# A decoder's mixer and sliding attentions: half weight tiles spread over eight steps, three engines' programs reordered, and the sliding attention's output product started beside its last units

## The chip, the cores and the metric

The kernel runs on one core of a Trainium2 chip. The core has five engines that run their own programs and wait for each other by semaphores: TensorE (matmuls; PE in the profile, its weight loads PEld), VectorE (DVE), ScalarE (ACT), GpSimd (POOL) and SyncE (SP, which here issues the weight loads from memory). The metric is the device time of one execution in microseconds (us), the median of the runs of one kernel.

## What is computed

Two transformer blocks on 256 tokens of width 1024, all in 32-bit floats, with one weight matrix after the other streamed from memory. Two of its parts matter here. First the mixer's attention:

```python
def hybrid_mixer(h, w_in, ...):
    ...
    o_nsa = nsa_attention(...)                    # 8 heads, 2 groups of keys, selected + window + compressed keys
    o_fox = forgetting_attention(...)             # 8 heads, a bias that decays with distance
    y = jax.nn.sigmoid(gate_a) * (o_nsa @ w_up_nsa) + jax.nn.sigmoid(gate_b) * (o_fox @ w_up_fox)
    return y @ w_out
```

Here `gate_a` and `gate_b` are columns of `h @ w_in`, that is, products that don't depend on the attention. Second the sliding attention of the last layer:

```python
def swa_layer(h, k_sh, v_sh, wq, q_gain, sinks, wo):
    q = rms_norm((h @ wq).reshape(B, T, N_Q_HEADS, HEAD_DIM), q_gain) * (HEAD_DIM ** -0.5)
    return swa_sink_attention(q, k_sh, v_sh, sinks) @ wo
```

## The kernel before

**Weights.** They come in tiles of 256 columns or rows, 1 MB each, into a ring of four places (`feed`, issued by SyncE). Each half tile (128 x 1024) is split into a rounded part, which ScalarE copies out of the ring (`tile_hi`, L294), and the rest, which VectorE subtracts (`tile_lo`, L304). There are four places for split halves, so a half can be split once the half four before it has been multiplied. A product takes three matmuls (L344 to L346), and a half tile 24 of them. `heads_after` and `rests_after` issue such splits for all halves whose place is free once a given half is done.

**Attention.** `attention_stage` runs over units (four lanes of scores for 128 queries). There are 12 units in the mixer: four with 128 keys and four with 256 keys of the first kind, then two with 128 keys and two with 256 of the second. The sliding attention has four units with 128 keys and four with 256. The stage is a software pipeline: in step s the engines do

- TensorE: scores of unit s, transposes of the weights of unit s-2 (L979), values of unit s-3
- VectorE: scores plus bias and their maximum for unit s (in the text: combine), division by the sums for unit s-1 (L1063), the store of unit s-3's output as a pair of parts (L338, L339)
- ScalarE: exponentials of unit s (L1005), and the copy of unit s-2's transposed weights out of PSUM (L1022)

Each engine goes through its steps in the order in which they are written. In the mixer the last four tiles of the gates ride along as fillers, because TensorE has little to do in an attention: one whole tile of 48 matmuls in each of steps 0 to 3, between the scores and the transposes, copied out by ScalarE (L1011). One wait sets the pace around them: TensorE starts a filler only when the one before is copied.

`ahead` is the step at which the splits for the section that follows are issued. At the end of the stage stands a barrier of all engines (`nc.Block`, L929), and then `up_stage` in the mixer, or `out_stage` (`row_to_T`, four tiles into PSUM banks 4 to 7) after the sliding attention.

Of the kernel before, what the change touches and what calls it, by code (L numbers as in the profile page):

```python
# [23 lines left out]
P = 128  # L24
SEQ = 256
# [354 lines left out]


def col_to_natural(e, pe, g, src, bank):
# [11 lines left out]
def row_to_T(e, pe, g, src, k0, first, last):  # L394


    def chunk(w, k, m):
        return product(pe, e.ps[:, 4 + m // 2, span(m % 2, SEQ)], cut(w, ALL, span(m, P)), cut(src, ALL, k0 + k, ALL),
                       first and k == 0 and m % 2 == 0, last and k == 1 and m % 2 == 1)
# [86 lines left out]

def add_to_residual(e, dve, b, scale, last_tile):

# [5 lines left out]
    if scale == 1.0:  # L494
        x = dve.tensor_tensor(xs, e.ps[:, 4 + b, :], xs, ALU.add)  # L495
    else:
        x = dve.scalar_tensor_tensor(out=xs, in0=e.ps[:, 4 + b, :], scalar=scale, in1=xs, op0=ALU.mult, op1=ALU.add)
    x.then_inc(*e.sig("residual_added").one())
# [10 lines left out]

def tail_vector(e, dve, scale, outs, last_tile):  # L510


    for n in range(6 if outs else 4):
        if n < 4:
            add_to_residual(e, dve, n, scale, last_tile)
        if outs and n >= 2:
# [394 lines left out]

def attention_stage(e, units, follows, fillers=(), hT=None, beside=None):

# [10 lines left out]
         "values_ready", "values_stored", "filler_copied", "dve_step"))  # L924
    last_tile = max([g for g, _ in fillers], default=-1)
    DEPTH = min(3, n)
    ahead = min(len(fillers) + 1, n - 1) + beside.delay

    with nc.Block() as block, ExitStack() as stack:  # L929
        tag = nc.next_id()  # L930
# [20 lines left out]
        def _(pe):  # L951
            for step in range(n + 3):
# [30 lines left out]
                if 0 <= u < n:  # L983
# [9 lines left out]
                    for mm in lasts:  # L993
                        mm.then_inc(*values_ready.one(2 // len(lasts)))

        @block.scalar
        def _(act):
            for step in range(n + 2):
                if beside:
                    beside.first_scalar(act, step)  # L1000
                if step < n:
                    act.wait_ge(*max_ready.at(step + 1))
                    st = stat[:, step % 2]
                    for lane in range(4):
                        x = act.activation(summed(step)[:, lane], summed(step)[:, lane], ACT.Exp,  # L1005
                                           bias=st[:, 0, lane:lane + 1], accum_out=st[:, 1, lane:lane + 1])
                    x.then_inc(*sums_ready.one())
                if step < len(fillers):
                    g, dst = fillers[step]
                    tile_after(e, act, g)  # L1010
                    act.activation(dst, e.ps[:, 7, :], ACT.Copy).then_inc(*filled.one())  # L1011
                if step == ahead:
                    heads_after(e, act, 2 * follows)
                u = step - 2
                if u >= 0:
# [5 lines left out]
                    src = e.ps[:, 4:6, :].rearrange("p b n -> p (b n)")[:, 0:width]  # L1021
                    act.activation(pT[:, u % 2, 0:width], src, ACT.Copy).then_inc(*copied.one())  # L1022

        @block.vector
        def _(dve):
            link = Chain(dve, dve_chain)
            for step in range(n + 3):
# [16 lines left out]
                if beside:  # L1044
                    beside.vector(dve, step)
                if step < len(fillers):
                    rests_before(e, dve, fillers[step][0] + 1)
                if step == ahead:
# [18 lines left out]
                if 0 <= u < n:  # L1067
                    dve.wait_ge(*values_ready.at(2 * (u + 1)))
                    units[u].store(link, out_ap(u)).then_inc(*stored.one())

def mixer_section(e):
    nc = e.nc
    with ExitStack() as stack:
# [24 lines left out]
                        + [fox_unit(e, m, t, j) for t in range(TT) for j in range(2)], FIRST["up"],  # L1101
                        fillers=[(FIRST["gates"] + n - 1, m.ab[:, 2 * n + 2:2 * n + 4, :].rearrange("p m n -> p (m n)"))
                                 for n in range(FILLERS, 7)], hT=e.hT, beside=front)
        memory.raw, memory.sq = e.sq, queries
# [1886 lines left out]
def swa_section(e, kvT):  # L2991
    with ExitStack() as stack:
# [8 lines left out]
        last = swa_projections(e, s, kvT)  # L3001
        attention_stage(e, [swa_unit(e, s, t, j) for t in range(TT) for j in range(4)], FIRST["wo2"], beside=last)
        out_stage(e, "wo2", s.o, [("ln_mlp1", e.hT)])

# [407 lines left out]
```

## Time and profile before

| what | us |
|---|---|
| median of 3 runs | 1501.92 (1501.85 to 1503.39) |
| the profiled execution, its own time | 1512.18 |
| its span, first to last instruction | 1510.9 |
| mixer's attention, first scores to the first matmul of the up section | 312.75 to 393.06 |
| sliding attention, first scores to the first matmul of its output product | 1244.6 to 1295.36 |
| the output product's 192 matmuls | 1295.36 to 1318.63 |

The profile shows one execution. TensorE is busy for 94% of the span, so most of the kernel is bound by its matmuls; the two attentions are the places where it idles, and the change concerns only them.

### The profile page before, as it was taken

What the parts mean: (1) busy time and instruction counts of PE and PEld (TensorE: products, weight loads), DVE (VectorE), ACT (ScalarE), POOL (GpSimd) and SP (SyncE); (2) the same over time, 40 slices, a digit from 0 to 9 for tenths busy, and PEclk for the clock granted to TensorE, in tenths of its full rate; (3) what the DMA queues carried; (4) which work ended last, traced back from release to release, by engine and by line L of the source; (5) the groups of instructions that cost most, each with busy time, mean ns of one, the idle gap of its engine ahead of it and who ended that gap; (6) DMA issues with size and microseconds to landing.
All of it is one profiled execution on the core that took longest, in us unless ns stands there. A gap on an engine that the chain in (4) does not pass through costs nothing. (4 is left out here: it accounts for less than half of the span.)

```text
span 1510.9 us, 28880 instructions
## 1 busy us (share of the span) xinstructions
PE 1420.5 (94%) x12748; PEld 1361.9 (90%) x12748; DVE 951.8 (63%) x1303; ACT 713.4 (47%) x1096; POOL 7.1 (0%) x12
## 2 busy tenths in 40 slices
PE   7999999997899999999989978998999996889999
PEld 7999999895799899999988977888999984889999
DVE  4655666468675456555678864566656678466565
ACT  5444454355464455444538423444444555454443
POOL 0000000000000000000000010000000000000000
PEclk9999999998999999999989986999999997999999
DMA  6555545640344334555514300023554530335542
GB/s 256 205 196 185 183 154 196 250 169 1 131 177 168 126 126 168 198 193 172 191 57 171 140 3 30 29 85 140 183 207 168 196 112 1 140 140 189 202 168 84
DMA packets 33108, 222.47 MB, mean 147 GB/s; under 512 B 3879, under 2 KB 5295, under 8 KB 6616
## 3 DMA queue, kind: packets, MB, share of 16 engines
q1 hardware_dynamic: 31928, 219.57, 40.3%
q8 instruction: 100, 1.64, 0.4%
q10 hardware_dynamic: 1056, 1.07, 0.2%
q14 instruction: 24, 0.20, 0.0%
HBM read 219.54 MB, written 1.07 MB: 146 GB/s over the span
## 5 line engine op out<-in xcount | busy, mean ns | idle before, releaser
L304 DVE TENSOR_TENSOR tile_lo<-ring,tile_hi 128x1024 fp32r<-128x1024 f32 x396 | 476.1, 1223 | 321.9 <-ACT tile_hi L294 321.2
L294 ACT ACTIVATE tile_hi<-ring 128x1024 fp32r<-128x1024 f32 x396 | 408.3, 1054 | 293.4 <-PE ps L346 289.3
L344 PE MATMUL ps<-hT_hi,tile_hi 128*128 128x256 f32 x1664 | 472.7, 284 | 10.1 <-DVE hidden_lo L753 7.6
L345 PE MATMUL ps<-hT_lo,tile_hi 128*128 128x256 f32 x1664 | 469.1, 282 | 0.0
L346 PE MATMUL ps<-hT_hi,tile_lo 128*128 128x256 f32 x1664 | 468.8, 282 | 0.0
L344 PEld LDWEIGHTS ps<-hT_hi,tile_hi 128*128 128x128 f32 x1664 | 316.0, 190 | 16.6 <-DVE hidden_lo L753 8.0
L346 PEld LDWEIGHTS ps<-hT_hi,tile_lo 128*128 128x128 f32 x1664 | 316.2, 190 | 0.0
L345 PEld LDWEIGHTS ps<-hT_lo,tile_hi 128*128 128x128 f32 x1664 | 315.9, 190 | 0.0
L344 PE MATMUL ps<-hidden_hi,tile_hi 128*128 128x256 f32 x864 | 241.5, 280 | 0.0
L346 PE MATMUL ps<-hidden_hi,tile_lo 128*128 128x256 f32 x864 | 241.5, 280 | 0.0
L345 PE MATMUL ps<-hidden_lo,tile_hi 128*128 128x256 f32 x864 | 241.5, 280 | 0.0
L346 PEld LDWEIGHTS ps<-hidden_hi,tile_lo 128*128 128x128 f32 x864 | 164.1, 190 | 0.0
L345 PEld LDWEIGHTS ps<-hidden_lo,tile_hi 128*128 128x128 f32 x864 | 162.9, 188 | 0.0
L344 PEld LDWEIGHTS ps<-hidden_hi,tile_hi 128*128 128x128 f32 x864 | 162.2, 188 | 0.0
L709 ACT ACTIVATE hidden_hi<-hidden_whole 128x512 fp32r<-128x512 f32 x54 | 34.1, 632 | 116.2 <-DVE hidden_whole L740 67.3
L753 DVE TENSOR_TENSOR hidden_lo<-hidden_whole,hidden_hi 128x512 fp32r<-128x512 f32 x54 | 37.4, 692 | 40.6 <-ACT hidden_hi L709 30.6
L1005 ACT ACTIVATE scores<-scores,lane_stats 128x128 f32<-128x128 f32 (+3 forms) x80 | 35.5, 445 | 47.0 <-DVE lane_stats L1043 46.9
L979 PEld LDWEIGHTS ps<-const_sb,scores 128*128 128x128 f32 x120 | 17.7, 178 | 33.7 <-issue 25.7
L979 PE MATMUL ps<-const_sb,scores 128*128 128x128 f32 x120 | 23.1, 346 | 26.5 <-ACT weightsT L1022 18.2
L746 DVE TENSOR_TENSOR hidden_whole<-gate,token_scale 128x512 f32<-128x512 f32 x32 | 22.2, 693 | 37.5 <-ACT gate L706 37.5
L706 ACT ACTIVATE gate<-ps 128x512 f32<-128x512 f32 x32 | 19.1, 597 | 47.6 <-PE ps L346 47.6
L344 PE MATMUL ps<-y_turned,tile_hi 128*128 128x256 f32 x128 | 36.2, 283 | 1.9 <-DVE tile_lo L304 1.9
(459 smaller groups left out, 2134.9 us busy)
## 6 DMA issues: line engine op xcount, KB each, us to landing
ring<-stream SPq DMA_DIRECT2D x204, 1024.0 KB, 4.8
x_sb<-x SPq DMA_DIRECT2D x4, 256.0 KB, 4.1
bias<-f_dram ACTq DMA_DIRECT2D x1, 1024.0 KB, 8.2
fox_bias<-forget_dram SPq DMA_DIRECT2D x1, 1024.0 KB, 6.2
squares<-mem SPq DMA_DIRECT2D x1, 1024.0 KB, 4.8
out<-x_sb SPq DMA_DIRECT2D x4, 256.0 KB, 2.2
const_sb<-const SPq DMA_DIRECT2D x1, 577.0 KB, 9.6
small_sb<-small SPq DMA_DIRECT2D x1, 493.5 KB, 9.7
```

The lines of the kernel that those rows point to most:

```text
L294: act.activation(e.w_hi[:, n % SPLIT, :], e.ring[:, tile % RING, span(n % 2, HALF)], ACT.Copy).then_inc(e.tile_hi.handle, 1)
L304: dve.tensor_tensor(e.w_lo[:, n % SPLIT, :], e.ring[:, CUT[n // 2] % RING, span(n % 2, HALF)], e.w_hi[:, n % SPLIT, :].bitcast(F32), ALU.s ...
L344: pe.matmul(out, left[0], right[0], start=start, stop=False)
L345: pe.matmul(out, left[0], right[1], start=False, stop=False)
L346: return pe.matmul(out, left[1], right[0], start=False, stop=stop)
L706: act.activation(tmp[:, j % 2, :], e.ps[:, 2 * (j % 2), :], ACT.Relu).then_inc(*act_done.one())
L709: act.activation(slot(hid[0], j), whole[:, j % 2, :], ACT.Copy).then_inc(*hi_ready.one())
L746: link.done(dve.tensor_tensor(halves_of(both), halves_of(tmp[:, j % 2, :]), scale_pairs(e), ALU.mult))
L753: dve.tensor_tensor(slot(hid[1], j), both, slot(hid[0], j).bitcast(F32), ALU.subtract).then_inc(*hidden_ready.one())
L979: tr = pe.transpose(e.ps[:, 4 + at // 512, at % 512:at % 512 + P], s[:, u % DEPTH, lane, kb * P:(kb + 1) * P], const(e, "ident"))
L1005: x = act.activation(summed(step)[:, lane], summed(step)[:, lane], ACT.Exp, bias=st[:, 0, lane:lane + 1], accum_out=st[:, 1, lane:lane + 1])
```

## The change

In the mixer the fillers become eight half tiles in steps 0 to 7, and TensorE does its half tile at the end of a step, behind the values. ScalarE's step is turned around: copy of the last filler, copy of the transposed weights, one split, and then the exponentials. VectorE's split moves to the end of its step. `attention_stage` is shared, so ScalarE's new order holds in the sliding attention too.

```diff
@@ attention_stage, tensor @@
-                if step == len(fillers) and step >= 1:
-                    pe.wait_ge(*filled.at(step))
-                if step < len(fillers):
-                    if step >= 1:
-                        pe.wait_ge(*filled.at(step))
-                    col_to_T(e, pe, fillers[step][0], hT, 7)
...
+                if tail and step >= n:
+                    if step == n:
+                        pe.wait_ge(*max_ready.at(n))
+                    tail.tensor(pe, step - n)
+                if step == len(fillers) and step >= 1:
+                    pe.wait_ge(*filled.at(step))
+                if step < len(fillers):
+                    if step >= 1:
+                        pe.wait_ge(*filled.at(step))
+                    g, half, _ = fillers[step]
+                    half_col_to_T(e, pe, g, half, hT, 7)
@@ attention_stage, scalar @@
+                if 1 <= step <= len(fillers):
+                    g, half, dst = fillers[step - 1]
+                    multiplied(e, act, g, half)
+                    act.activation(dst, e.ps[:, 7, span(half, SEQ)], ACT.Copy).then_inc(*filled.one())
+                u = step - 2
+                if u >= 0:
+                    act.wait_ge(*turned.at(u + 1))
...
+                    act.activation(pT[:, u % 2, 0:width], src, ACT.Copy).then_inc(*copied.one())
+                if step < len(fillers):
+                    g, half, dst = fillers[step]
+                    heads_after(e, act, 2 * g + half)
                 if step < n:
                     act.wait_ge(*max_ready.at(step + 1))
@@ attention_stage, vector @@
-                if step < len(fillers):
-                    rests_before(e, dve, fillers[step][0] + 1)
...
                     units[u].store(link, out_ap(u)).then_inc(*stored.one())
+                if step < len(fillers):
+                    rests_after(e, dve, 2 * fillers[step][0] + fillers[step][1])
```

After the sliding attention the first three half tiles of the output product `wo2` are multiplied in the drain of the pipeline, steps 8 to 10, one behind the values of each step; they need only the units whose outputs are already stored. They go to banks 0 to 3, which the last scores have left, and the barrier between the two is gone (`Open` instead of `nc.Block`). The rest follows in a new `swa_output`:

```diff
+class SlidingOutput:
...
+    def half_tile(self, pe, i, k):
+        e = self.e
+        pe.wait_ge(*self.stored.since(5 + i))
+        w = arrived(e, pe, FIRST["wo2"] + i, k)
+        for m in range(KC):
+            mm = product(pe, e.ps[:, m // 2, span(m % 2, SEQ)], cut(w, ALL, span(m, P)), cut(self.o, ALL, 2 * i + k, ALL),
+                         i == 0 and k == 0 and m % 2 == 0, False)
+        mm.then_inc(*e.tile_done.one())
+
+    def tensor(self, pe, n):
+        self.half_tile(pe, n // 2, n % 2)
@@ swa_output @@
+            for n in range(3, 6):
+                rest.tensor(pe, n)
+            pe.wait_ge(*stored.since(8))
+            row_to_T(e, pe, g0 + 3, s.o, 6, False, True, 0)
```

The changed order, at three places. ScalarE in the mixer, from the exponentials of unit 0 on, before:

```order
L294 ACTIVATE tile_hi<-ring 128x1024
L1011 ACTIVATE gates_ab<-ps 128x512
L1005 ACTIVATE scores,lane_stats<-scores,lane_stats 128x128 x4
L294 ACTIVATE tile_hi<-ring 128x1024 x2
L1011 ACTIVATE gates_ab<-ps 128x512
L1022 ACTIVATE weightsT<-ps 128x512
L1005 ACTIVATE scores,lane_stats<-scores,lane_stats 128x128 x4
```

and in the changed kernel (its lines have other numbers; `gates_ab` is the copied filler):

```order
L1018 ACTIVATE gates_ab<-ps 128x256
L294 ACTIVATE tile_hi<-ring 128x1024
L1035 ACTIVATE scores,lane_stats<-scores,lane_stats 128x128 x4
L1018 ACTIVATE gates_ab<-ps 128x256
L1027 ACTIVATE weightsT<-ps 128x512
L294 ACTIVATE tile_hi<-ring 128x1024
L1035 ACTIVATE scores,lane_stats<-scores,lane_stats 128x128 x4
```

A step now has one split instead of two, in front of the exponentials instead of behind them, and the copy of the transposed weights has moved in front of them as well.

VectorE in the mixer, around the end of step 3 and step 4, before:

```order
L1536 TENSOR_TENSOR scores<-ps,bias 128x2x128 x2
L1043 TENSOR_REDUCE lane_stats<-scores 128x4
L304 TENSOR_TENSOR tile_lo<-ring,tile_hi 128x1024 x2
L1054 RECIPROCAL lane_stats<-lane_stats 128x4
L1058 TENSOR_TENSOR lane_stats<-lane_stats,gate_nsa 128x4
L1063 TENSOR_SCALAR scores<-scores,lane_stats 128x128 x4
```

and in the changed kernel:

```order
L1553 TENSOR_TENSOR scores<-ps,bias 128x2x128 x2
L1060 TENSOR_REDUCE lane_stats<-scores 128x4
L1069 RECIPROCAL lane_stats<-lane_stats 128x4
L1073 TENSOR_TENSOR lane_stats<-lane_stats,gate_nsa 128x4
L1078 TENSOR_SCALAR scores<-scores,lane_stats 128x128 x4
L338 CAST o_parts<-ps 128x128
L339 TENSOR_TENSOR o_parts<-ps,o_parts 128x128
L304 TENSOR_TENSOR tile_lo<-ring,tile_hi 128x1024
```

The subtraction for the split has moved from between the maximum and the division to the end of the step.

TensorE at the end of the sliding attention (transposes L979, values L3224), before:

```order
L979 MATMUL ps<-const_sb,scores 128x128 x8
L3224 MATMUL ps<-weightsT,v_swa 64x128 x8
L979 MATMUL ps<-const_sb,scores 128x128 x8
L3224 MATMUL ps<-weightsT,v_swa 64x128 x16
L929 UNCONDITIONAL_BRANCH
```

and in the changed kernel, from the first half tile's last matmul (there are 24 matmuls in front of these rows that read `o_swa`):

```order
L346 MATMUL ps<-o_swa_hi,tile_lo 128x256
L982 MATMUL ps<-const_sb,scores 128x128 x8
L3293 MATMUL ps<-weightsT,v_swa 64x128 x8
L344 MATMUL ps<-o_swa_hi,tile_hi 128x256
...
L346 MATMUL ps<-o_swa_hi,tile_lo 128x256
L3293 MATMUL ps<-weightsT,v_swa 64x128 x8
L344 MATMUL ps<-o_swa_hi,tile_hi 128x256
```

A half tile of the output product now stands between the values of unit 5 and the transposes of unit 7, one between the values of units 6 and 7, and there is no branch to a barrier.

## Rows read from the trace of the kernel before

**Rows 1.** The page, busy time (share of the span) and instructions.

```profile
PE 1420.5 (94%) x12748; PEld 1361.9 (90%) x12748; DVE 951.8 (63%) x1303; ACT 713.4 (47%) x1096; POOL 7.1 (0%) x12
```

**Rows 2.** Stretches of the mixer: length, PE, PEld, DVE, ACT, POOL busy, PEclk, DMA.

```profile
312.75:340.83 28.08, 28.00 (x246) 26.42 (x245) 17.02 (x32) 16.57 (x45) 0.00 (x0) 1.00 0.40 146
340.83:366.50 25.67, 16.85 (x122) 11.42 (x120) 21.14 (x55) 11.76 (x38) 0.00 (x0) 0.73 0.00 1
366.50:393.06 26.56, 17.84 (x172) 13.63 (x173) 18.59 (x53) 13.34 (x41) 0.00 (x0) 0.87 0.00 1
354.00:362.00 8.00, 5.65 (x28) 3.77 (x28) 6.98 (x20) 2.75 (x10) 0.00 (x0) 0.50 0.01 2
```

**Rows 3.** Waits, 312 to 394: who for whom, total us, times, longest.

```profile
DVE tile_lo L304 <- ACT tile_hi L294: 13.8, 5, 3.1
PE ps L979 <- ACT weightsT L1022: 9.8, 7, 2.9
```

**Rows 4.** Timeline of VectorE, mixer: start, us, operation [idle before].

```profile
315.13 0.73 DVE L1536 TENSOR_TENSOR scores<-ps,bias 128x256 f32<-128x256 f32 x2
315.90 0.69 DVE L1043 TENSOR_REDUCE lane_stats<-scores 128x4 f32<-128x512 f32 x1
319.26 1.23 DVE L304 TENSOR_TENSOR tile_lo<-ring,tile_hi 128x1024 fp32r<-128x1024 f32 x1 [2.67 <-ACT tile_hi L294]
...
356.70 1.28 DVE L1536 TENSOR_TENSOR scores<-ps,bias 128x512 f32<-128x512 f32 x2
...
359.15 0.17 DVE L1054 RECIPROCAL lane_stats<-lane_stats 128x4 f32<-128x4 f32 x1
...
360.61 0.29 DVE L338 CAST o_parts<-ps 128x128 fp32r<-128x128 f32 x1
...
366.50 0.76 DVE L1581 TENSOR_TENSOR scores<-ps,cmp_in 128x256 f32<-128x256 f32 x2
```

**Rows 5.** Timeline of ScalarE, mixer.

```profile
323.46 2.00 ACT L294 ACTIVATE tile_hi<-ring 128x1024 fp32r<-128x1024 f32 x2
326.04 0.60 ACT L1011 ACTIVATE gates_ab<-ps 128x512 f32<-128x512 f32 x1 [0.59 <-PE ps L346]
329.52 0.40 ACT L1005 ACTIVATE scores<-scores,lane_stats 128x128 f32<-128x128 f32 x1 [2.88 <-DVE lane_stats L1043]
...
361.25 1.00 ACT L1022 ACTIVATE weightsT<-ps 128x1024 f32<-128x1024 f32 x1
```

**Rows 6.** Timeline of TensorE, mixer.

```profile
344.96 1.13 PE L1530 MATMUL ps<-k_sel_win,queries 64*128 64x256 f32 x8
...
367.72 1.06 PE L979 MATMUL ps<-const_sb,scores 128*128 128x128 f32 x8 [1.26 <-ACT weightsT L1022]
368.71 1.09 PE L1546 MATMUL ps<-weightsT,v_sel_win 128*64 128x128 f32 x16
369.74 0.43 PE L1548 MATMUL ps<-cmp_weightsT,cmp_v 15*64 15x128 f32 x4
```

**Rows 7.** Busy time by stretch, end of the sliding attention and its output product.

```profile
1286.00:1290.00 4.00, 3.96 (x27) 3.44 (x28) 0.55 (x3) 1.02 (x1) 0.00 (x0) 0.57 0.00 0
1295.36:1318.86 23.50, 23.27 (x193) 23.10 (x193) 10.24 (x12) 8.96 (x13) 0.00 (x0) 1.00 0.62 218
```

**Rows 8.** Timelines of the sliding attention, three engines.

```profile
1256.06 1.11 PE L979 MATMUL ps<-const_sb,scores 128*128 128x128 f32 x4
1256.75 0.41 ACT L1005 ACTIVATE scores<-scores,lane_stats 128x129 f32<-128x129 f32 x1 [3.29 <-DVE lane_stats L1043]
...
1259.38 1.23 DVE L304 TENSOR_TENSOR tile_lo<-ring,tile_hi 128x1024 fp32r<-128x1024 f32 x1 [2.02 <-ACT tile_hi L294]
...
1284.04 0.42 DVE L338 CAST o_swa_hi<-ps 128x256 fp32r<-128x256 f32 x1
...
1286.04 1.91 PE L979 MATMUL ps<-const_sb,scores 128*128 128x128 f32 x8 [3.06 <-ACT weightsT L1022]
...
1295.36 0.36 PE L344 MATMUL ps<-o_swa_hi,tile_hi 128*128 128x256 f32 x1 [1.25 <-PEq L929]
```

More of the change, by code:

```diff
@@ L379, in col_to_T, with half_col_to_T @@
             between()
+def half_col_to_T(e, pe, g, half, src, bank):
+    w = chunks_of(arrived(e, pe, g, half))
+    for k in range(KC):
+        mm = product(pe, e.ps[:, bank, span(half, SEQ)], cut(w, ALL, k, ALL), cut(src, ALL, k, ALL), k == 0, k == KC - 1)
+    mm.then_inc(*e.tile_done.one())
 def col_to_natural(e, pe, g, src, bank):
@@ L909, in keys_of, with attention_stage @@
     return n, slice(SEQ - n, SEQ)
-def attention_stage(e, units, follows, fillers=(), hT=None, beside=None):
+def attention_stage(e, units, follows, fillers=(), hT=None, beside=None, tail=None):
     e.stage()
@@ L1045, in _ @@
                     beside.vector(dve, step)
-                if step < len(fillers):
-                    rests_before(e, dve, fillers[step][0] + 1)
                 if step == ahead:
@@ L1101, in mixer_section @@
                         + [fox_unit(e, m, t, j) for t in range(TT) for j in range(2)], FIRST["up"],
-                        fillers=[(FIRST["gates"] + n - 1, m.ab[:, 2 * n + 2:2 * n + 4, :].rearrange("p m n -> p (m n)"))
-                                 for n in range(FILLERS, 7)], hT=e.hT, beside=front)
+                        fillers=[(FIRST["gates"] + n - 1, half, m.ab[:, 2 * n + 2 + half, :])
+                                 for n in range(FILLERS, 7) for half in range(2)], hT=e.hT, beside=front)
         memory.raw, memory.sq = e.sq, queries
@@ L3001, in swa_section, with __init__, swa_output, _ @@
         last = swa_projections(e, s, kvT)
-        attention_stage(e, [swa_unit(e, s, t, j) for t in range(TT) for j in range(4)], FIRST["wo2"], beside=last)
-        out_stage(e, "wo2", s.o, [("ln_mlp1", e.hT)])
+        attention_stage(e, [swa_unit(e, s, t, j) for t in range(TT) for j in range(4)], FIRST["wo2"], beside=last, tail=SlidingOutput(e, s))
+        swa_output(e, s)
+class SlidingOutput:
+    def __init__(self, e, s):
+        self.e, self.o, self.stored = e, s.o, e.sig("values_stored")
+    def half_tile(self, pe, i, k):
[5 more added lines that the diff above has]
+                         i == 0 and k == 0 and m % 2 == 0, False)
+        mm.then_inc(*e.tile_done.one())
+    def tensor(self, pe, n):
+        self.half_tile(pe, n // 2, n % 2)
+def swa_output(e, s):
+    e.stage()
+    g0 = FIRST["wo2"]
+    outs = [("ln_mlp1", e.hT)]
+    stored = e.sig("values_stored")
+    rest = SlidingOutput(e, s)
+    with Open(e.nc) as block:
+        @block.sync
+        def _(sp):
+            feed(e, sp, g0 + 4)
+        @block.tensor
+        def _(pe):
+            mark_tail(e)
+            for n in range(3, 6):
+                rest.tensor(pe, n)
+            pe.wait_ge(*stored.since(8))
+            row_to_T(e, pe, g0 + 3, s.o, 6, False, True, 0)
+        @block.scalar
+        def _(act):
+            heads_after(e, act, 2 * (g0 + 3))
+            tail_scalar(e, act, outs, then=lambda: heads_after(e, act, 2 * (g0 + 4)))
+        @block.vector
+        def _(dve):
+            rests_after(e, dve, 2 * (g0 + 3))
+            tail_vector(e, dve, 1.0, outs, g0 + 3, 0)
+            rests_after(e, dve, 2 * (g0 + 4))
 def swa_projections(e, s, kvT):
```

40 lines of the change are left out of this document (19 added, 21 removed).

## The prediction

> **What bounds the kernel now.** I read the page's busy times first: TensorE is busy for 94% of the span [rows 1], so time can only be won where it idles. The busy times by stretch then show where that is in the mixer's attention. From 312.75 to 340.83 TensorE is busy for 28.00 of 28.08 us at the full clock: these are steps 0 to 3, each with a whole filler tile. From 340.83 to 366.50, steps 4 to 7, it is busy for 16.85 of 25.67 us although its clock is down to a mean 0.73, and VectorE for 21.14 [rows 2]. So the stage has two halves with opposite limits, and the work that would fill the second lies in the first. The list of waits names the price: VectorE waits five times, 13.8 us in all, for ScalarE's `tile_hi` [rows 3]. The timelines show why. The subtraction stands in VectorE's program right behind the maximum, ScalarE does its exponentials (4 x 0.39) and then one or two splits (2.00 us for two), and VectorE stands still for 2.67 us with the division and the next combine queued behind it [rows 4, 5]. The next wait in size is TensorE's transposes for ScalarE's copy of the transposed weights, 9.8 us, since that copy waits behind the exponentials [rows 3].
>
> **The change in the mixer, steps 0 to 7.** Nothing is removed: the fillers are the same 192 matmuls. 192 matmuls of the same size take 23.27 us, 0.121 each, so a half tile takes 2.9 [rows 7]. The copy of a filler doubles in number and halves in width: 0.60 us for the whole [rows 5], taken as 0.4 each, between the 0.3 of half the work and the whole 0.6; ScalarE has room for either.
>
> One step with 256 keys now costs TensorE scores 1.1, transposes 1.0, values 1.1 + 0.3 (0.43 less its overlap) and the filler 2.9: 6.4 [rows 6]. The values have half as many matmuls until unit 4, about 0.5 less. It costs VectorE the combine 2.45 (356.70 to 359.15), the division 1.46 (359.15 to 360.61), a store 0.6 and a subtraction 1.15 to 1.2: 5.7 [rows 4]. ScalarE has 0.4 + 1.0 + 1.04 + 2.0 = 4.4. The two busiest engines are thus almost even, at about 6 us a step.
>
> Adding VectorE's program from the first combine (315.13) to that of step 8: combines 4 x 1.5 + 4 x 2.45 = 15.8; divisions 4 x 1.2 + 3 x 1.46 = 9.2; five stores 3.0; seven subtractions 8.1; together 36.1. To these come its waits, which I placed by going through the steps engine by engine with these durations. In step 1 TensorE cannot start filler 1 (316.9) before ScalarE has done exponentials 0 (318.2) and the copy (318.6): 1.7 us of TensorE, and that delays scores 2, for which VectorE waits 1.4. The other waits for scores are 0.5, 0.3, 1.1 in steps 1, 3, 4 and 0.7 later. Sum 4.0. Step 8's combine then starts at 315.13 + 40.1 = 355.2, where before it started at 366.50 [rows 4]: 11.3 us earlier. The subtraction no longer waits: its split is made in front of the exponentials, and VectorE comes to it only after the combine, division and store, 4.5 us in.
>
> **The mixer, from step 8 on.** It took 26.56 us before [rows 2]. Two things move here. The last split for the up section now falls into step 9, and it still stands behind the exponentials on ScalarE, so VectorE's wait of 2.8 us and the 1.15 of its subtraction come along: +4.0, with the division of unit 8 and everything after it queued behind. The transposes of the last units no longer wait for a copy that stands behind the exponentials (in the whole stage 9.8 us of such waits [rows 3]). Going through steps 8 to 14 with the same durations I get 26.2 us from step 8's combine to the up section, so the drain gives 4.3 back. Net -0.3. The clock was at half between 354 and 362 [rows 2], behind a stretch where TensorE did little. In the new drain I find it idle for nearly 4 us around the split of step 9, so I put 1.1 us (one set of transposes) on it; the bounds are 0 and 2.5, the transposes and values of one unit. The mixer's gain is 11.3 + 0.3 - 1.1 = 10.5, with bounds of 8.5 and 12.
>
> **The sliding attention, cost first.** ScalarE's new order holds there too, and at step 2 it speaks against the change. The transposes of unit 0 end at 1257.17 while the exponentials of unit 2 started at 1256.75 [rows 8]. Now they wait for those transposes and for the copy (0.6): 1.05 later. The split of that step stands behind the exponentials, and VectorE waits for it at 1259.38 (2.02 us), so the whole 1.05 reaches VectorE, with the division of unit 1 queued behind.
>
> **Its gain.** VectorE has finished the division of unit 6 at 1284.04, yet the transposes of unit 6 start at 1286.04, since a copy stands behind the exponentials of unit 7 [rows 8]. They then run at half clock: 1.91 for what takes 1.06, with a granted clock of 0.57 from 1286 to 1290 [rows 6, 7, 8]. In the new order they start at 1284.04 + 1.0 = 1285.0, with nearly all of the 1.05 arriving here, since VectorE is busy without a break in between (an estimate). From there TensorE never waits: transposes 6 and 7 2 x 1.05, values 5 to 7 3 x 1.05, eight half tiles 8 x 2.9 (all of the product, the last tile's two included), which makes 28.6, to 1313.6. The next section began at 1318.86 with 0.2 of waiting, so the product ended at 1318.6 [rows 7]: 5.0 us. The three halves that fill the drain weigh 8.7; the rest is lost because the values of units 6 and 7 now stand behind them. Stores are hidden: that of unit 7 (0.9) lies beside 14 us of halves. Splits for halves 4 to 7 start when half 0 is done and have 8 us in hand. The barrier (1.25 behind PEq [rows 8]) mostly overlapped the last store (0.9): 0.3, contained in the sum. The first half tile may fall into the stretch at half clock, which then costs up to 2.9; I take 0.5. Gain 4.5, bounds 2 and 6.
>
> **The clock.** The granted clock stays 1.00 where TensorE is dense and is 0.50 after the thin stretch of steps 5 and 6 [rows 2]. The Trainium skill's TensorE: Matmul & The Clock Gate, What's actually happening, says that the throttled clock is the default and that activity releases it. By that rule alone steps 4 to 7 keep the full clock once they are dense, which is what the sum assumes, and if they stay thin they take rival (c)'s price, +26. The trace agrees with the rule as far as it goes: it shows both a dense and a thin stretch.
>
> **Sum.** 10.5 + 4.5 = 15.0 off the profiled execution's own 1512.18, which is 1% of it; the median of the runs is 0.7% lower, which changes 15.0 by 0.1. 1501.92 - 15.0 = 1487.0. No change in other sections is counted: their orders are the same.
>
> **Rivals.** (a) The drain halves of the sliding attention give nothing. They push the values of units 6 and 7 back (2 x 2.9), the first two halves run at 1.2 GHz (+2.9 each at most), and the 1.05 at step 2 stays: gain 0 to 1, and 1501.9 - 10.5 - 0.5 = 1491. For it: 1286 to 1290 was at half clock. Against it: the new order is denser in front of it.
>
> (b) The fillers' copies become the chain. TensorE waits for the copy of the last filler, which stands behind that step's exponentials. If the 1.7 us of step 1 came back in all eight steps, 13.6 would go: 1500. Against it: from step 2 on scores, transposes and values (2 to 3.5 us) stand between the two, more than the wait.
>
> (c) Slower: TensorE's clock falls in the mixed steps. A half tile at 1.2 GHz takes 5.8, and a step's 6.4 becomes 12.8. Steps 4 to 7 at half clock would cost 4 x (12.8 - 6.4) = 26, so 1487 + 26 = 1513; it decides from 60% of these steps on. For it: the clock was at 0.50 just there. Against it: in those steps TensorE was busy for 2.9 us fewer each; with the half tile its longest idle stretch in steps 0 to 7 is the 1.7 in step 1.
>
> (d) The half-clock stretches vanish in both stages altogether and the drain runs full: 12 + 6, 1484.
>
> **Chances and range.** My forecast (1482 to 1491, with (d) in it) 0.74; (a) down to 1493 0.12; (b) 0.06, of which half lies within 0.2% (3 us, about what a measurement of this kernel can tell from no change); (c) 0.03; something unseen in other sections 0.05, either way. Range 1482 to 1493. Faster 0.92, the same 0.05, slower 0.03.
>
> **What would show it.** In the profile after: the waits of VectorE for `tile_hi` in the mixer fall from five (13.8) to one of about 2.8 in step 9; the granted clock in steps 4 to 7 is 1.00; the first combine of the second kind of units starts 40 us behind the first combine; the whole stage is 68 to 72 us long instead of 80.3. In the sliding attention VectorE's wait for its one split grows from 2.02 to 3.1, the transposes of unit 6 start 27 to 29 us before the product's end, and no L929 stands between values and product. I am wrong if TensorE waits for `gates_ab` in most steps, if the clock drops in the first eight steps, or if the transposes of unit 7 come so late that VectorE's last stores delay the last tile.

## The result and the profile after

| what | before | after |
|---|---|---|
| median of 6 runs each, us | 1501.38 (1499.71 to 1503.39) | 1488.91 (1483.43 to 1494.34) |
| mixer's attention, first scores to the up section | 80.31 | 70.91 |
| of it: first combine to step 8's combine | 51.37 | 40.36 |
| of it: step 8's combine to the up section | 26.56 | 28.17 |
| sliding attention, first scores to the next section (product included) | 74.24 | 70.53 |

The changed kernel takes 0.9915 of the time before, with a 95% interval of 0.9886 to 0.9943: 12.5 us less by the medians, and 8.6 to 17.1 by the interval. The rows of the table below the first are from one profiled execution of each kernel. The two stages together give 9.40 + 3.71 = 13.1 us.

The profiled execution after took 1490.88 us. That is 21.3 less than that of before, and 8.2 us of this lie where nothing was changed: before the mixer's attention (1.8), between the two attentions (2.7) and behind the second (3.7). The section on the hardware comes back to it.

Busy time on the page after, in answer to [rows 1]. TensorE has the same 12748 matmuls and is busy with them for 10 us less; ScalarE has four more copies.

```profile
PE 1410.4 (95%) x12748; PEld 1352.0 (91%) x12748; DVE 951.4 (64%) x1303; ACT 714.6 (48%) x1100; POOL 7.1 (0%) x12
```

Busy time by stretch in the mixer's attention after, in answer to [rows 2] (length, PE, PEld, DVE, ACT, POOL, granted clock, DMA share, GB/s): steps 0 to 7, then the drain in three pieces.

```profile
310.99:353.73 42.74, 41.30 (x366) 35.50 (x366) 37.14 (x86) 29.11 (x86) 0.00 (x0) 1.00 0.24 83
353.73:363.60 9.87, 6.53 (x72) 4.90 (x72) 6.86 (x21) 6.05 (x19) 0.00 (x0) 1.00 0.00 0
363.60:370.00 6.40, 6.34 (x38) 4.22 (x38) 5.33 (x15) 2.67 (x9) 0.00 (x0) 0.53 0.00 0
370.00:381.90 11.90, 7.23 (x66) 5.59 (x65) 7.31 (x21) 4.72 (x11) 0.00 (x0) 0.82 0.01 1
```

What TensorE did in 53.75 us before (28.08 dense and 25.67 thin, 368 matmuls) is now done in 42.74 us (366), evenly and at the full clock. What is left of the idle time lies in the drain, and so does the half clock: 6.40 us at 0.53.

The list of waits in the mixer's attention after, in answer to [rows 3] (who for whom, total, times, longest):

```profile
ACT weightsT L1027 <- PE ps L982: 16.3, 12, 3.1
...
DVE scores L1553 <- PE ps L1547: 4.1, 6, 1.4
...
DVE tile_lo L304 <- ACT tile_hi L294: 2.8, 1, 2.8
...
PE ps L344 <- ACT gates_ab L1018: 1.4, 1, 1.4
```

VectorE's five waits for a split are one, and TensorE no longer waits for the copied weights; ScalarE waits for the transposes instead, which costs nothing in these steps, since TensorE is busy for 41.30 of these 42.74 us and VectorE for 37.14.

### The profile page after: what moved, and what is told of

Same layout as the page of the kernel before. It is cut to its first block and busy times, and to the rows that moved or that the text cites. A ratio compares the mean times of both kernels' runs of the same rounds, so it can differ in the third digit from the quotient of the medians.

```text
span 1489.6 us, 28884 instructions
## 1 busy us (share of the span) xinstructions
PE 1410.4 (95%) x12748; PEld 1352.0 (91%) x12748; DVE 951.4 (64%) x1303; ACT 714.6 (48%) x1100; POOL 7.1 (0%) x12
## 5 line engine op out<-in xcount | busy, mean ns | idle before, releaser
L754 DVE TENSOR_TENSOR hidden_whole<-gate,token_scale 128x512 f32<-128x512 f32 x32 | 22.2, 693 | 37.7 <-ACT gate L714 37.7
L709 ACT ACTIVATE gate<-gate 128x512 f32<-128x512 f32 x22 | 13.9, 632 | 46.8 <-DVE gate L742 46.8
L346 PE MATMUL ps<-y_turned,tile_lo 128*128 128x256 f32 x128 | 35.8, 279 | 0.0
```

Source lines behind the costliest of these rows:

```text
L346: return pe.matmul(out, left[1], right[0], start=False, stop=stop)
L754: link.done(dve.tensor_tensor(halves_of(both), halves_of(tmp[:, j % 2, :]), scale_pairs(e), ALU.mult))
```

## The experiments

**The same kernel once more**, to see how much of the profile belongs to the execution and how much to the kernel.

> The changed kernel once more, for its time and its stages in a second execution, since its six runs lay 11 us apart and those of before 4. Stages are measured in the trace: the mixer's attention from the first scores to the first matmul of the up section (70.9 in the first execution, 80.3 before), the sliding attention with its output product from the first scores to the next section's first matmul (70.5, 74.2 before). Theory: the stages come out within 1 us of that again and the scatter lies elsewhere; ratio to before 0.990 to 0.993. Rival: the scatter is in these two stages, by TensorE's clock; then one of them moves by 2 us or more.

1489.83 us (6 runs), ratio 0.9904 [0.9872, 0.9936]. The mixer's attention took 70.95 us and its parts 40.35 and 28.21, all within 0.05 of the first time. The sliding attention took 68.59 instead of 70.53. That the drains agree is in part chance. Cut at the transposes of unit 10 (step 12), they took 19.50 and 8.71 us, the first time 19.17 and 9.00, at a mean granted clock of 0.76 instead of 0.82. So a difference of 0.3 us in steps 0 to 7 says something, one of 1 us in the mixer's drain or of 2 us in the sliding attention does not by itself.

**Whole filler tiles in the new order**, the sliding tail undone: is it the order or the halves?

```diff
-                    g, half, dst = fillers[step - 1]
-                    multiplied(e, act, g, half)
-                    act.activation(dst, e.ps[:, 7, span(half, SEQ)], ...)
+                    g, dst = fillers[step - 1]
+                    multiplied(e, act, g)
+                    act.activation(dst, e.ps[:, 7, :], ...)
...
-        attention_stage(e, [swa_unit(...) ...], FIRST["wo2"], beside=last, tail=SlidingOutput(e, s))
-        swa_output(e, s)
+        attention_stage(e, [swa_unit(...) ...], FIRST["wo2"], beside=last)
+        out_stage(e, "wo2", s.o, [("ln_mlp1", e.hT)])
```

> Four whole filler tiles in steps 0 to 3 again, but with the new orders of TensorE, ScalarE and VectorE (two splits in front of the exponentials); in the sliding attention ScalarE's new order, and the output product behind the barrier as before. Theory (both parts of the mixer's change are needed): steps 0 to 3 are bound by TensorE as before, steps 4 to 7 by VectorE, and the two splits at step 5 behind the exponentials cost 6 us; the mixer stage takes 76 us, against 70.9 with half tiles. Rival: the order alone does it, 71 to 72. Sliding attention: the drain is shorter by the copy that no longer waits, 2 us less than before, 72; rival: the new order costs there what it gains (1.05 at step 2), 74.

1497.93 us (10 runs), ratio 0.9955 [0.993, 0.9979]. The mixer's attention took 77.36 us (76 expected). Its first eight steps took 50.99, against 51.37 before: the order gives them nothing when the tiles are whole. The drain took 23.99 against 26.56 before: no split falls into it in either, so these 2.6 us are what the new order gives there. In the sliding attention the order alone took 72.78 us. Busy time by stretch of this kernel, steps 4 to 7, shows [rows 2] again, with the half clock in it:

```profile
341.00:366.26 25.26, 16.84 (x121) 11.78 (x122) 19.55 (x46) 13.67 (x39) 0.00 (x0) 0.73 0.00 1
```

**Half tiles in the old order**, with the sliding tail: half tiles in front of the transposes, splits and copies behind the exponentials (whose last line is the first of the diff), VectorE's split behind the maximum.

```diff
@@ scalar, one step @@
+                    x.then_inc(*sums_ready.one())
+                if step < len(fillers):
+                    g, half, dst = fillers[step]
+                    heads_after(e, act, 2 * g + half)
+                    multiplied(e, act, g, half)
+                    act.activation(dst, e.ps[:, 7, span(half, SEQ)], ACT.Copy).then_inc(*filled.one())
@@ vector, behind the maximum @@
+                if step < len(fillers):
+                    rests_after(e, dve, 2 * fillers[step][0] + fillers[step][1])
```

> Eight half tiles in eight steps, but all orders as before: the filler between scores and transposes, ScalarE's exponentials first, its split and the two copies behind them, VectorE's subtraction behind the maximum. The sliding attention has ScalarE's old order with the new product beside its last units. Theory: VectorE waits in each of seven steps 2.7 to 3.1 us for the split, so that its steps take 6.5 to 8.8; the mixer stage takes 85 to 89 us, longer than before (80.3), and the change without its order would be a loss. Rival: spreading alone gives most of it, 72 to 75. Sliding attention: transposes 6 wait for the copy behind exponentials 7 as before, and from there TensorE is full, 28.6 us: 71 to 72.

1507.73 us (10 runs), ratio 1.0023 [0.9995, 1.005]. The mixer's attention took 88.95 us, 8.6 more than before: 5.3 in the first eight steps and 3.3 in the drain, into which the last split has moved. The sliding one took 72.07. The waits of this kernel in the mixer's attention, and then VectorE's timeline there (start, duration, operation, idle before):

```profile
ACT scores L1019 <- DVE lane_stats L1058: 39.6, 11, 5.0
DVE tile_lo L304 <- ACT tile_hi L294: 23.0, 8, 3.1
...
PE ps L344 <- ACT gates_ab L1026: 10.2, 6, 2.9
```

```profile
321.60 0.75 DVE L1551 TENSOR_TENSOR scores<-ps,bias 128x256 f32<-128x256 f32 x2
322.39 0.69 DVE L1058 TENSOR_REDUCE lane_stats<-scores 128x4 f32<-128x512 f32 x1
325.74 1.23 DVE L304 TENSOR_TENSOR tile_lo<-ring,tile_hi 128x1024 fp32r<-128x1024 f32 x1 [2.66 <-ACT tile_hi L294]
326.88 0.17 DVE L1069 RECIPROCAL lane_stats<-lane_stats 128x4 f32<-128x4 f32 x1
```

VectorE gives the maximum, waits until ScalarE has done four exponentials and a split, and only then goes on; ScalarE meanwhile waits for the next maximum (39.6 us). The two take turns in all eight steps instead of four. Rival (b)'s wait is there as well, six times and 10.2 us. Half tiles without the order are thus worse than nothing (+8.6), the order without half tiles gives 3.0, and both give 9.4.

**The last split in front of the exponentials**, and its subtraction at the end of VectorE's step.

```diff
@@ scalar: in front of the exponentials, was behind them @@
+                if step == ahead:
+                    heads_after(e, act, 2 * follows)
@@ vector: at the end of the step, was behind the maximum @@
+                if step == ahead:
+                    rests_after(e, dve, 2 * follows)
```

> The changed kernel with one thing more: the last split (step 9 of the mixer, step 2 of the sliding attention) stands in front of the exponentials too, and VectorE's subtraction for it at the end of its step. Theory: VectorE's wait of 2.8 us in the mixer and of 2.95 in the sliding attention goes, and nothing else is as late there: mixer 68.1, sliding attention 67.6, 5 to 6 us less in all. Rival: the exponentials, now 1.04 later, are waited for instead, so that half or less is won (mixer 69.5 or more, sliding 69 or more).

1482.12 us (6 runs), ratio 0.9854 [0.9817, 0.9891]. The mixer's attention took 66.84: 40.40 for the steps and 24.06 for the drain, which is 4.1 less than in the changed kernel. The sliding one took 65.40. Busy time by stretch of this kernel, steps and drain, and VectorE's timeline at the sliding attention's split:

```profile
310.12:352.90 42.78, 41.34 (x366) 35.54 (x366) 37.09 (x86) 29.12 (x86) 0.00 (x0) 1.00 0.27 97
352.90:376.96 24.06, 17.18 (x172) 12.96 (x173) 19.37 (x53) 13.23 (x39) 0.00 (x0) 0.93 0.00 1
```

```profile
1238.61 1.23 DVE L304 TENSOR_TENSOR tile_lo<-ring,tile_hi 128x1024 fp32r<-128x1024 f32 x1 [0.43 <-ACT tile_hi L294]
```

The wait of 2.81 is gone and the clock in the drain is 0.93. I had expected 68.1 for the stage, and it took 1.3 less; the clock came on top of the wait: in the changed kernel VectorE waits another 0.93 us for scores that TensorE gives at half clock (the section on the prediction has the row), and that wait is gone too.

**The clock held by matmuls that nobody reads.** Nothing of the computation changes: 22 and 10 matmuls of the identity by itself go into a bank that is free then, at the start of steps 10 and 12, and 14 and 16 in the sliding attention.

```diff
+                keep_busy(e, pe, hold.get(step, 0), 7)
...
+                        ..., beside=front, hold={10: 22, 12: 10})
...
+        attention_stage(..., tail=SlidingOutput(e, s), hold={6: 14, 8: 16})
```

> The changed kernel with matmuls on the identity, whose result nobody reads, put into TensorE's idle stretches: 22 in step 10 and 10 in step 12 of the mixer's attention, 14 in step 6 and 16 in step 8 of the sliding attention, each before the transposes for which TensorE waits anyway (3.4, 1.9, 2.1 and 2.6 us of idle time; 22 take about 2.9 us). Theory: the clock at half after those stretches costs 1 to 2 us in each stage; held at 1.00 the mixer takes 69.5 to 70 (70.9 in both executions of the change) and the sliding attention 68 to 68.6 (70.5 and 68.6). Rival: the half clock lies beside VectorE's work and costs nothing, both stages unchanged to 0.3.

One execution, 1490.24 us. The mixer's attention took 69.09 us and its drain 26.27 instead of 28.17. Busy time by stretch of this kernel in the drain:

```profile
355.11:381.38 26.27, 23.00 (x236) 19.04 (x237) 19.47 (x53) 13.46 (x39) 0.00 (x0) 1.00 0.00 1
```

The clock stays at 1.00, and that is worth 1.9 us here, although the added matmuls were mispriced: each of them is two instructions in the trace, so that 22 ran for 5.18 us and not for 2.9, longer than the gap of 3.40 that they were to fill. The transposes behind them started 11.5 us after the combine of step 8, where they had started after 9.9. In the sliding attention I expected 68.0 to 68.6 and measured 69.93. TensorE's timeline of this kernel shows why:

```profile
1268.15 3.84 PE L354 MATMUL ps<-const_sb 128*128 128x128 f32 x32
1271.83 1.04 PE L983 MATMUL ps<-const_sb,scores 128*128 128x128 f32 x8
```

The block of 16 outlasts its gap as well, and the transposes of unit 6 start 41.1 us behind the first scores instead of 40.1. From there to the next section it takes 28.8 us, in the changed kernel 30.4. So the full clock is worth 1.6 us there, and 1.0 of it goes into the overlong block.

**Another bank for the second filler**, so that it need not wait for the copy of the first.

```diff
-                    if step >= 1:
+                    if step >= 2:
                         pe.wait_ge(*filled.at(step))
                     g, half, _ = fillers[step]
-                    half_col_to_T(e, pe, g, half, hT, 7)
+                    half_col_to_T(e, pe, g, half, hT, 6 if step == 1 else 7)
```

> The changed kernel with filler 1 in PSUM bank 6 (free until the first values), so that TensorE need not wait in step 1 for the copy of filler 0, which stands behind the exponentials of unit 0. Theory: the 1.44 us that TensorE waited there go, and with them VectorE's 1.35 in step 2; the combine of step 8 comes 39.0 us behind the first instead of 40.4, the mixer takes 69.5. Rival: VectorE is the bound of the first eight steps and has the same work to do, so that the wait only moves to a later step: unchanged 40.4 and 70.9.

One execution, 1486.82 us. The steps took 39.07 instead of 40.36, as expected, and the drain 27.09 instead of 28.17, which was not. VectorE's timeline of this kernel has its combine of unit 2 without a wait, and TensorE's timeline has the same gap in the drain as the changed kernel, but less of the half clock behind it (values 1.27, where the changed kernel shows 1.98 below):

```profile
318.29 0.75 DVE L1553 TENSOR_TENSOR scores<-ps,bias 128x256 f32<-128x256 f32 x2
```

```profile
361.55 0.66 PE L982 MATMUL ps<-const_sb,scores 128*128 128x128 f32 x4 [3.40 <-DVE scores L1078]
362.17 1.27 PE L1563 MATMUL ps<-weightsT,v_sel_win 128*64 128x128 f32 x16
```

So the 1.1 us of the drain are not the bank's: the work behind the gap met the half clock a little later.

**The sliding attention's part alone**: the mixer keeps a copy of the stage's program as it was before.

```diff
-        attention_stage(e, [nsa_unit(e, m, t, i) ...
+        attention_stage_before(e, [nsa_unit(e, m, t, i) ...
```

> The mixer's attention as before the change, the sliding attention with its new order and the output product beside its last units. Theory: mixer 80.3, sliding attention 68.6 to 70.5, the whole 3.7 to 5.6 us less than before (ratio 0.9963 to 0.9975). Rival: the part is worth nothing by itself, ratio above 0.999.

1501.75 us (12 runs) beside 1506.03 for the kernel before (17 runs), ratio 0.9974 [0.9952, 0.9996]: 3.9 us, with 0.6 to 7.2 by the interval. The mixer's attention took 80.30 (before 80.31) and the sliding one 70.51 (after 70.53). The two parts of the change don't touch each other.

**All three additions together**, with added matmuls of 18 in the mixer's step 12 and of 14 and 16 in the sliding attention.

> The changed kernel with the last split in front of the exponentials, filler 1 in the other bank, and matmuls on the identity in step 12 of the mixer (18) and steps 6 and 8 of the sliding attention (14 and 16). Theory: 66.8 less 1.4 for the bank less 1 for the clock, 64.4 for the mixer; 65.4 less 0 to 1 for the sliding attention, 64.9; the whole 7 us less than the changed kernel, ratio to before 0.983 to 0.985. Rival: VectorE binds, mixer 66.8 as with the split alone.

1482.79 us (6 runs), ratio 0.9845 [0.9811, 0.9878]. Mixer 65.56, sliding 66.39, which is 1.2 and 1.5 more than expected. The next kernel shows why.

**The same without the added matmuls.**

> The last split in front of the exponentials and filler 1 in the other bank, without the matmuls on the identity. Theory: the two savings add, since one lies in steps 1 and 2 and the other in step 9: 66.8 less 1.4 = 65.5 for the mixer's attention; the sliding attention 65.4, as with the split alone, because the matmuls on the identity cost there 1.0 (66.4 with them); ratio to before 0.984. Rival: the matmuls on the identity are needed for the clock, mixer 66.5 or more, sliding 66.4 or more.

1480.74 us (5 runs) beside 1504.33 (9 runs), ratio 0.9839 [0.9816, 0.9861]. Mixer 65.53, sliding 66.94. This is faster than the kernel before by 24 us, and by the medians 8 to 9 us faster than the changed one. It has the lowest ratio of all, but the three kernels with the moved split (0.9854, 0.9845, 0.9839) are not told apart by their intervals. Busy time by stretch in the mixer's drain, cut at the transposes of unit 10, first with the added matmuls and TensorE's timeline around them, then without:

```profile
350.17:366.49 16.32, 14.90 (x152) 12.03 (x153) 15.74 (x44) 11.18 (x37) 0.00 (x0) 1.00 0.00 1
366.49:374.27 7.78, 4.81 (x59) 3.84 (x57) 3.64 (x11) 2.05 (x2) 0.00 (x0) 0.97 0.00 0
```

```profile
362.37 4.29 PE L354 MATMUL ps<-const_sb 128*128 128x128 f32 x36
366.49 1.04 PE L983 MATMUL ps<-const_sb,scores 128*128 128x128 f32 x8
```

```profile
350.06:365.30 15.24, 10.86 (x117) 7.92 (x117) 14.82 (x41) 10.39 (x34) 0.00 (x0) 1.00 0.00 1
365.30:374.13 8.83, 6.33 (x56) 5.03 (x57) 4.56 (x13) 2.83 (x6) 0.00 (x0) 0.81 0.00 0
```

The two drains take as long, 24.10 and 24.07, but not because the half clock costs nothing. The full clock saves 1.05 us behind the transposes of unit 10 (7.78 instead of 8.83), and the added block, 4.29 us in a gap of 2.96, makes them start 1.08 us later (16.32 instead of 15.24).

The same two things part the sliding attentions, for which 65.4 was expected. With the added matmuls the transposes of unit 6 start 37.6 us behind the first scores and not 36.6, and this 1.0 is the difference between 66.39 and the 65.40 of the split's own run. Without them they start at 36.6, as in that run, but then the clock decides. TensorE's timeline, first here (66.94) and then in the split's own run (65.40), the transposes of unit 6, the values behind them and the transposes of unit 7:

```profile
1258.42 1.09 PE L982 MATMUL ps<-const_sb,scores 128*128 128x128 f32 x8 [2.58 <-DVE scores L1076]
1259.44 1.59 PE L3293 MATMUL ps<-weightsT,v_swa 128*64 128x128 f32 x16
...
1264.96 1.04 PE L982 MATMUL ps<-const_sb,scores 128*128 128x128 f32 x8
```

```profile
1260.99 1.09 PE L982 MATMUL ps<-const_sb,scores 128*128 128x128 f32 x8 [2.58 <-DVE scores L1076]
1262.01 1.09 PE L3293 MATMUL ps<-weightsT,v_swa 128*64 128x128 f32 x16
...
1266.00 1.03 PE L982 MATMUL ps<-const_sb,scores 128*128 128x128 f32 x8
```

Behind the same gap of 2.58 us the transposes, the values and the half tile took 6.5 us in one execution (mean granted clock 0.74 from 1258.42 to 1264.96) and 5.0 in the other (1.00), and that is the whole difference.

## Why the prediction came out right, and where it was off

1487.0 was forecast, and 1488.91 and 1489.83 were measured, inside the range of 1482 to 1493. The likeliest case was the one that happened. Six runs of one kernel lie 10 to 11 us apart, so that the total comes out within 2 to 3 us is in part luck; what bears the prediction out are its single steps:

**Steps 0 to 7 of the mixer: right.** The sum was 36.1 of work and 4.0 of waits, 40.1, and 40.36 was measured, both times. The waits stand where they were placed, VectorE's timeline after shows them (start, duration, operation, idle before), the combines of steps 1, 2, 4 and 8:

```profile
315.44 0.76 DVE L1553 TENSOR_TENSOR scores<-ps,bias 128x256 f32<-128x256 f32 x2 [0.61 <-PE ps L1547]
...
320.60 0.76 DVE L1553 TENSOR_TENSOR scores<-ps,bias 128x256 f32<-128x256 f32 x2 [1.35 <-PE ps L1547]
...
330.26 1.29 DVE L1553 TENSOR_TENSOR scores<-ps,bias 128x512 f32<-128x512 f32 x2 [1.28 <-PE ps L1547]
...
353.73 0.76 DVE L1598 TENSOR_TENSOR scores<-ps,cmp_in 128x256 f32<-128x256 f32 x2 [0.44 <-PE ps L1592]
...
361.38 1.22 DVE L304 TENSOR_TENSOR tile_lo<-ring,tile_hi 128x1024 fp32r<-128x1024 f32 x1 [2.81 <-ACT tile_hi L294]
```

Forecast were 0.5, 1.4 and 1.1, and 2.8 for the one split that is left (the last row). That the 1.35 comes from TensorE's stall for the copy of filler 0 (1.44; forecast 1.7) is shown by the other bank, which takes both away and 1.3 us with them.

**From step 8 on: the split and the drain right, the clock too small.** I had 26.56 + 4.0 (split) - 4.3 (drain) + 1.1 (clock) = 27.4, and it took 28.17. The terms can be told apart when each drain is cut at the transposes of unit 10, which wait for VectorE's last division but one:

| kernel | step 8's combine to these transposes | from there to the up section |
|---|---|---|
| before | 17.09 | 9.47 |
| changed | 19.17 | 9.00 |
| changed, clock held | 18.44 | 7.83 |
| whole tiles, new order | 14.41 | 9.58 |
| last split in front | 15.22 | 8.84 |
| all three additions | 16.32 | 7.78 |

Busy time by stretch of the second part, before, changed and with the clock held, and of both parts with whole tiles, where no split falls into the drain:

```profile
383.59:393.06 9.47, 6.97 (x56) 5.59 (x57) 3.30 (x9) 2.05 (x2) 0.00 (x0) 0.75 0.01 2
372.90:381.90 9.00, 6.18 (x57) 4.89 (x57) 4.48 (x14) 2.84 (x6) 0.00 (x0) 0.81 0.00 0
373.55:381.38 7.83, 4.86 (x56) 3.89 (x57) 4.47 (x13) 2.85 (x6) 0.00 (x0) 1.00 0.00 0
366.26:380.67 14.41, 10.85 (x117) 7.91 (x117) 13.77 (x41) 9.60 (x34) 0.00 (x0) 0.94 0.00 0
380.67:390.25 9.58, 7.08 (x56) 5.62 (x57) 4.56 (x13) 2.84 (x6) 0.00 (x0) 0.74 0.01 2
```

The second part takes 7.8 us at a mean clock of 0.97 to 1.00 and 8.8 to 9.6 at a mean of 0.74 to 0.81. A drain without a split and at full clock is then 14.41 + 7.78 = 22.2 us, an estimate from two kernels, and 22.3 is what I had walked to (26.56 - 4.3). The split, with the clock held, adds 18.44 - 14.41 = 4.0, as forecast. The clock is 28.17 - 26.27 = 1.9 and not 1.1 (bounds 0 and 2.5). That makes 26.56 - 4.4 + 4.0 + 1.9 = 28.1. So the term that was too small is the clock. One set of transposes was put for it, but the half clock costs at two places: VectorE waits 0.93 us for the scores of step 11 (0.21 with the clock held), and the second part is 1.2 us longer. That the three drains without a wait for a split all take 24.0 to 24.1 is a coincidence: one has the half clock (9.58), one some of it and the subtraction in step 9 (15.22), one the overlong added block (16.32).

TensorE's timeline after shows what came before it fell:

```profile
363.66 0.79 PE L982 MATMUL ps<-const_sb,scores 128*128 128x128 f32 x4 [3.40 <-DVE scores L1078]
364.39 1.98 PE L1563 MATMUL ps<-weightsT,v_sel_win 128*64 128x128 f32 x16
```

and VectorE's what follows from it, the combine of step 11:

```profile
369.04 1.29 DVE L1598 TENSOR_TENSOR scores<-ps,fox_bias 128x512 f32<-128x512 f32 x2 [0.93 <-PE ps L1592]
```

TensorE does nothing for 3.40 us, since the division that it waits for is queued behind the subtraction on VectorE, which waits for the split; then values that take 1.09 at full clock take 1.98. So one misplaced split costs 4.1 us (28.17 - 24.06): 2.81 for the wait, 0.93 for the scores at half clock, and 0.4 in smaller pieces, of which 0.2 lie behind the transposes of unit 10. The Trainium skill's TensorE: Matmul & The Clock Gate, HAM oscillation — how this bites in real kernels, tells the same of a loop that waits for its transfers: each idle gap makes the next batch start throttled. The trace agrees, with a gap that comes from VectorE instead (clock 1.00 before and in it, 0.53 behind it). Not every gap does it: behind the 2.58 us shown above the clock was at half in one execution and at full in another. The mixer's gain was 9.4 instead of 10.5, inside its bounds of 8.5 and 12: 0.8 of the difference is the clock, 0.3 the first eight steps.

**The sliding attention: the steps and the drain right, the clock too small again.** VectorE's wait for its split grew from 2.02 to 2.95 (forecast 3.1), as its timeline after shows:

```profile
1246.43 1.23 DVE L304 TENSOR_TENSOR tile_lo<-ring,tile_hi 128x1024 fp32r<-128x1024 f32 x1 [2.95 <-ACT tile_hi L294]
```

The transposes of unit 6 started 40.1 us behind the first scores (forecast 40.4). TensorE's timeline after, from there:

```profile
1270.83 1.09 PE L982 MATMUL ps<-const_sb,scores 128*128 128x128 f32 x8 [2.59 <-DVE scores L1078]
1271.86 1.89 PE L3293 MATMUL ps<-weightsT,v_swa 128*64 128x128 f32 x16
1273.67 0.58 PE L344 MATMUL ps<-o_swa_hi,tile_hi 128*128 128x256 f32 x1
...
1301.25 0.35 PE L344 MATMUL ps<-hT_hi,tile_hi 128*128 128x256 f32 x1 [0.23 <-DVE hT_lo L513]
```

From 1270.83 to 1301.02, the product's end, are 30.2 us, where 28.6 + 0.5 were forecast. The values of unit 5 (1.89 instead of 1.09) and the first half tile, 3.7 us until the transposes of unit 7 at 1277.39 where 2.9 was put, ran at half clock in part: 1.6 us for the 0.5. The 30.2 also lies outside the 27 to 29 us named as a sign. The 28.6 itself (its terms as printed add to 28.5) is right: it was 28.6 in each of four executions in which the clock was at 1.00 there, namely the second one of this kernel and those with the clock held, with the split in front and with all three additions. In the second execution the transposes also started 0.4 us earlier, and the whole gain was 5.65. So 3.7 and 5.65 stand around the forecast 4.5. Busy time by stretch after confirms the full drain: from unit 7's transposes on TensorE waits for nothing.

```profile
1274.00:1277.40 3.40, 3.40 (x25) 3.40 (x25) 0.66 (x2) 0.00 (x0) 0.00 (x0) 0.79 0.00 0
1277.40:1301.25 23.85, 23.62 (x211) 22.80 (x209) 11.76 (x16) 9.87 (x14) 0.00 (x0) 1.00 0.35 124
```

What the two edits give there, apart (to the transposes of unit 6, and from there to the next section):

| kernel | to the transposes | from there | together |
|---|---|---|---|
| neither | 41.4 | 32.8 | 74.24 |
| the order alone | 40.1 | 32.7 | 72.78 |
| the halves in the drain alone | 41.7 | 30.4 | 72.07 |
| both | 40.1 | 30.4 | 70.53 |

The halves take 2.3 to 2.4 us off the second column, of the 8.7 us of work that they carry forward. That the rest is lost, as the forecast said, is borne out: from these transposes to the next section TensorE needs 28.8 us even at full clock, so that of the 32.8 no more than 4.0 can go. The order gives 1.3 to 1.5; of the 1.05 that it costs at step 2, 0.93 does come, and is more than given back. The whole differences are about as large as the 2 us between two executions of one kernel, but all four of these had the half clock behind the transposes of unit 6, so that they can be compared, and the parts repeat within 0.3 us. The two edits together are also borne out by the runs of the sliding part alone.

**The rivals.** (a), that the drain halves give nothing, is out by the mechanism (TensorE is busy in 23.62 of the last 23.85 us) and nearly so by the times. (b) showed its wait once in eight steps, 1.44 us, and six times in the old order, where the copies do stand behind the exponentials. (c) was the dangerous one, and the clock was at 1.00 in all of the mixed steps. (d), the full clock, put the gains at 12 and 6. With the clock held they were 11.2 and 4.3, or 5.3 without the overlong block there. So it was the better description of what a full clock would bring, and in the changed kernel itself it did not happen.

**The sum.** 10.5 + 4.5 = 15.0 against 9.4 + 3.7 = 13.1 in the trace and 12.5 by the medians, both inside the interval. The two terms for the clock, 1.1 and 0.5, measured 1.9 and 1.6; these 1.9 us are the difference between 15.0 and 13.1, and the other errors, 0.3 each, cancel.

## What to carry to other kernels

When two engines work through a step in turns (maximum, exponentials, a split for both), cutting the filler work smaller does not help by itself: it made this stage 8.6 us longer, 5.3 of them in the steps with the fillers, until whatever only serves a later section was moved in front of the exponentials on the one engine and to the end of the step on the other, so that neither waits for the other with its main work queued behind. Spread filler work over the thin steps until each engine has about the same in every step, and then look at what is left once behind the old place: one split left there cost 4.1 us here, about as much as the whole change of the second stage brought. An idle gap on TensorE is to be priced with the matmuls behind it, not only with its own length: here 1.9 and 1.6 us. Matmuls that only fill such a gap must be shorter than it is. In the kernel with all three additions they were too long by about 1 us at each of two places, where the full clock gave back 1.05 and 1.5 us.

## What the runs showed of the hardware

The runs of one kernel lie further apart than one stage's gain: 1483.4 to 1494.3 for the changed one, 1494.6 to 1513.0 for the one before in its 23 runs beside the first experiments. The trace shows one place of it, in the long middle between the attentions, whose programs are the same in all kernels and which took 843.3 to 851.6 us. Busy time by stretch over 40 us there, at the same distance from the span's start, first in the changed kernel's first profiled execution and then in its second:

```profile
901.90:941.90 40.00, 36.83 (x361) 31.87 (x360) 19.64 (x26) 14.78 (x38) 1.04 (x2) 0.85 0.08 28
```

```profile
901.90:941.90 40.00, 37.01 (x378) 31.93 (x376) 22.70 (x27) 15.19 (x41) 1.04 (x2) 0.94 0.08 28
```

TensorE is busy as long in both but does 17 matmuls more in the second, at a granted clock of 0.94 instead of 0.85, although its middle had begun 1.9 us later. The same gaps let the clock fall in one execution and not, or for a shorter time, in another; the sliding attention's first half tile (3.7 and 3.0 us) is the same thing in small. A gain of 2 us in a stage behind such a gap can't be claimed from one execution. The mixer's attention is not free of it, though it took 70.91 and 70.95: the half clock lay at other places of its drain the second time (19.50 + 8.71 instead of 19.17 + 9.00), and the sums agree by chance. Which executions keep the full clock behind a gap stays open.
